# Mixer gate pieces on split weights, and the last two units' numerators ahead of the output-gate tiles

## What is computed

```python
mod = (jax.nn.silu(cond) @ ada_w + ada_b).astype(x.dtype).reshape(cond.shape[0], N_MOD, 1, D_MODEL)
sh1, sc1, gt1, sh2, sc2, gt2 = [mod[:, i] for i in range(N_MOD)]
h = rms_norm(x, norm_g[0]) * (1 + sc1) + sh1
y, st = mixer_sublayer(h, st, w_in, ...)
x = x + gt1 * rms_norm(y, norm_g[1])
h = rms_norm(x, norm_g[2]) * (1 + sc2) + sh2
a = dwconv_centred(h @ ffn_up, ffn_conv)
val, gate = jnp.split(a, 2, axis=-1)
y = (jax.nn.silu(gate) * val) @ ffn_down
x = x + gt2 * rms_norm(y, norm_g[3])
```

## Time and profile before

| what | value |
|---|---|
| device time, median of 3 runs | 873.22 us (873.04 to 874.27) |
| profiled execution: device time | 871.22 us |
| profiled execution: span | 869.5 us |
| mean granted TensorE clock | 0.976 of full speed |
| PE busy | 821.0 us, 94% of the span |
| PEld, DVE, ACT, POOL busy | 724.7, 531.2, 350.8, 86.1 us |
| line 1486 (unsplit gate pieces) in the chain that ended last | 2% of the span |

### The profile page before, as it was taken

One profiled execution on the slowest core, in us unless ns is written; L12 is line 12 of the kernel. 1 busy time (PEld: TensorE's weight loads), 2 busy tenths in 40 slices (PEclk: granted clock), 3 DMA queues, 4 the chain that ended last, 5 costly groups with the idle time before them and its releaser, 6 DMA issues.

```text
span 869.5 us, 13027 instructions
## 1 busy us (share of the span) xinstructions
PE 821.0 (94%) x4891; PEld 724.7 (83%) x4891; DVE 531.2 (61%) x763; ACT 350.8 (40%) x555; POOL 86.1 (10%) x118
## 2 busy tenths in 40 slices
PE   3679999999999979899999999999999999999996
PEld 2569999988976568659999999999999958888785
DVE  3873185797868557896555555555565564445854
ACT  3683252323111224783434343424333343335542
POOL 2630003121210026120000000000000000000000
PEclk8789999999999989999999999999999999999999
DMA  9872117578514684454222323132222063332662
GB/s 294 276 205 73 49 51 206 148 131 156 164 55 121 194 271 129 145 145 123 73 76 69 93 58 91 51 94 72 72 72 72 24 217 121 121 121 98 215 207 85
DMA packets 99951, 109.54 MB, mean 126 GB/s; under 512 B 7000, under 2 KB 79864, under 8 KB 99656
## 3 DMA queue, kind: packets, MB, share of 16 engines
q1 hardware_dynamic: 94103, 95.77, 36.7%
q0 software_dynamic: 3952, 11.53, 5.2%
q10 hardware_dynamic: 1856, 1.71, 0.6%
HBM read 106.19 MB, written 2.82 MB: 125 GB/s over the span
## 4 chain that ended last, share of the span: by engine, by line
PE 83%; DVE 7%; DMA 5%; issue 3%; ACT 3%; SPq 0%; ACTq 0%; DVEq 0%
PE PAIR L1530 47%; PE PAIR L1707 21%; PE PAIR L1540 3%; PE PAIR L1486 2%; DMA RAW<-in_ada_w_dram 2%; PE PAIR L1501 2%; DVE WLO L1030 2%; ACT WHI L790 1%; PE PAIR L1667 1%; PE PAIR L1643 1%; PE PAIR L1662 1%; DMA RAW<-in_w_out_dram 1%; PE PAIR L1678 1%; DVE T L1387 1%; DMA RAW<-in_w_in_dram 1%
## 5 line engine op out<-in xcount | busy, mean ns | idle before, releaser
L1530 PE MATMUL PAIR<-Hhi,WHI 128*128 128x320 f32 x960 | 224.7, 313 | 4.5 <-DVE Hlo L1370 3.5
L1530 PE MATMUL PAIR<-Hlo,WHI 128*128 128x320 f32 x960 | 222.5, 310 | 0.0
L1530 PE MATMUL PAIR<-Hhi,WLO 128*128 128x320 f32 x960 | 222.4, 310 | 0.0
L1030 DVE TENSOR_TENSOR WLO<-RAW,WHI 128x1024 fp32r<-128x1024 f32 (+1 forms) x115 | 146.4, 1284 | 61.9 <-ACT WHI L790 57.1
L1530 PEld LDWEIGHTS PAIR<-Hhi,WHI 128*128 128x128 f32 x960 | 161.9, 189 | 6.6 <-issue 6.3
L1530 PEld LDWEIGHTS PAIR<-Hlo,WHI 128*128 128x128 f32 x960 | 162.6, 189 | 0.0
L1530 PEld LDWEIGHTS PAIR<-Hhi,WLO 128*128 128x128 f32 x960 | 162.2, 189 | 0.0
L790 ACT ACTIVATE WHI<-RAW 128x1024 fp32r<-128x1024 f32 (+1 forms) x115 | 119.1, 1049 | 41.7 <-DMA RAW<-in_ada_w_dram 14.4
L1707 PE MATMUL PAIR<-WHI,ASHI 128*128 128x512 f32 x300 | 95.9, 401 | 9.7 <-DVE GATE L1081 5.1
L1707 PE MATMUL PAIR<-WLO,ASHI 128*128 128x512 f32 x300 | 95.3, 399 | 0.0
L1707 PE MATMUL PAIR<-WHI,ASLO 128*128 128x512 f32 x300 | 95.2, 399 | 0.0
(11 more groups left out here) (218 smaller groups left out, 835.8 us busy)
## 6 DMA issues: line engine op xcount, KB each, us to landing
RAW<-in_ada_w_dram SPq DMA_DIRECT2D x48, 512.0 KB, 4.5
RAW<-in_ffn_up_dram SPq DMA_DIRECT2D x44, 512.0 KB, 3.7
RAW<-in_ffn_down_dram SPq DMA_DIRECT2D x44, 512.0 KB, 3.3
RAW<-in_w_in_dram SPq DMA_DIRECT2D x20, 512.0 KB, 4.8
RAW<-in_w_out_dram SPq DMA_DIRECT2D x16, 512.0 KB, 5.2
WE<-weight_rows POOLq DMA_DIRECT2D x20, 128.0 KB, 4.8
out_dram<-X SPq DMA_DIRECT2D x5, 512.0 KB, 5.6
X<-in_x_sample_dram POOLq DMA_DIRECT2D x4, 512.0 KB, 6.0
```

The source lines that it names most:

```text
L1030: dve.tensor_tensor(WLO[:, u % RING, 0:w], RAW[:, u % RING, 0:w], WHI[:, u % RING, 0:w].bitcast(F32), ALU.subtract).then_inc(lo_split, 1)
L1530: last = pe.matmul(t[:, 512 * half:512 * half + HALF], w[:, n_or_slot, cols(k)], h[:, k, HALF * half:HALF * half + HALF], start=(k == 0 an ...
```

## The change

Units of pieces 4 and 5 are no longer raw: ScalarE and VectorE split all eight, and TensorE runs `split_rows` on them (16 matmuls of 512 columns for each piece, CONDHL by WHI and WLO). Pieces 10 and 11 stay as they were. In PLAN the steps behind `pl 1` are put in another order: `p2 4` and `ada 5` come first, then `C 8` and `C 9`, then both output-gate tiles. VectorE's product for `o 0`, which stood behind `C 9`, is now in step `o 0`. Step `p2 5` moves into the output projection, behind its third chunk, and uses PAIR3. By the rule of turns, `ada 4` still has PAIR0, `p2 4` now has PAIR0, `ada 5` PAIR1, `o 0` PAIR0 and `o 1` PAIR1.

What the splitting steps are given follows from `goal`: step `ad 11` now splits the first two units of piece 4 (50 and 51, in the list of all units), step `pz 1` the third (52), step `ada 4` the fourth (53) and three units of piece 5 (54 to 56), step `ada 5` the last of piece 5 (57), both output-gate tiles' (58, 59) and the first of the output projection (60). Before, `ad 11` and `pz 1` had nothing to split, `ada 4` one unit (`o 0`), and `ada 5` three.

```diff
-    ("B", 9), ("pl", 1), ("C", 8), ("o", 0), ("p2", 4), ("ada", 5), ("C", 9), ("o", 1), ("p2", 5)]
+    ("B", 9), ("pl", 1), ("p2", 4), ("ada", 5), ("C", 8), ("C", 9), ("o", 0), ("o", 1)]
...
-PLAN_OUT = (k_steps(0, KC) + [("epi", 0)] + B_OUT[0:1] + [("epi", 1), ("nrm", 0)] + B_OUT[1:2] + [("nrm", 1)]
+A_OUT = k_steps(0, KC)
+PLAN_OUT = (A_OUT[0:3] + [("p2", 5)] + A_OUT[3:] + [("epi", 0)] + B_OUT[0:1] + [("epi", 1), ("nrm", 0)] + B_OUT[1:2] + [("nrm", 1)]
...
-            ("out", "ada", 10): 2, ("out", "p2", 10): 2, ("down", "ada", 11): 0, ("down", "p2", 11): 0}
+            ("out", "p2", 5): 3, ("out", "ada", 10): 2, ("out", "p2", 10): 2, ("down", "ada", 11): 0, ("down", "p2", 11): 0}
...
         def raw_unit(n):
-            return UNITS[n][0] == "ada"
+            return UNITS[n][0] == "ada" and UNITS[n][1] > 5
...
             def ada(key, p):
-                take_rows(key, 512, key[:-2] + ("p2", p))
+                take_rows(key, 512, ("p2", 4) if p == 4 else ("out", "p2", p) if p < 11 else ("down", "p2", p))
...
                         last.then_inc(c_read, 1)
                         dve.wait_ge(c_read, UPD.index((g, d)) + 1)
-                    if n == len(MUNITS) - 1:
-                        output_gate(0)
...
-                elif kind == "o" and n:
+                elif kind == "o":
                     output_gate(n)
...
             def split_rows(s):
...
-                n = len(AD_BLOCKS[s[1]])
+                n = 4 if s[0] == "ada" else len(AD_BLOCKS[s[1]])
...
             def mix(s):
                 kind, n = s
-                if kind == "ada":
-                    ada(s, UPTO[s] - 4)
-                elif kind == "ad":
+                if kind in ("ada", "ad"):
                     split_rows(s)
...
                 elif s[0] == "p2":
-                    piece2(("out",) + s, ("out", "ada", s[1]))
+                    piece2(("out",) + s, ("ada", 5) if s[1] == 5 else ("out", "ada", s[1]))
```

## The result

The change makes the kernel slower: 876.37 us against 873.49 us, medians of 20 runs each, 2.9 us apart. The ratio is 1.0041 with a 95% interval of 1.0025 to 1.0057, some 3.6 us, and so far apart are the means too: five of the twenty runs after took 880.3 to 882.1 us, the others 874.0 to 878.1. Forecast were 873.6 us, 870.1 to 875.9, and "no change" as the likeliest case. The profiled execution after took 875.58 us (span 873.8, mean granted clock 0.975 against 0.976); it is not one of those five.

What follows compares the result with a forecast made beforehand. TensorE was taken as the bound (83% of the span), so its waits and work count. Gone 13.4 us, new waits and half clock 13.4, some 0.3 for hand-overs: net +0.3, 873.6 us, range 870.1 to 875.9.

Steps and rivals of the forecast that it cites:

- The three waits: New TensorE waits: 1.55 us before `pz 1`, about 6.8 inside piece 4, 2.2 before piece 5.
- The output gap: TensorE's 5.08 us idle before the output projection, forecast to go.
- the gap and its restart: Output projection start: 5.08 us of idle time and 1.85 lost at half clock behind it, both forecast to go.
- Step `ada 4`: Piece 4: TensorE waits about 6.8 us for unit 53's split, then restarts at half clock for 4.0 us, 1.9 lost.
- the bound of 3.0: Behind the 6.8 us wait: half clock costs between nothing and all of 3.15 + 0.93 halved, about 3.0 us.
- Step `ada 5`: Piece 5: TensorE waits 2.2 us for ScalarE's copy of PAIR1, then 0.9 for unit 57's split.
- the second one (0.9): Inside piece 5, after three quarters: TensorE waits 0.9 us for VectorE's split of unit 57.
- the second fall: Rival: clock falls at the wait before `ada 5`, piece 5 and unit 8 lose 1.5 us: 875.1; chance 0.15.
- What it removes: Pieces 4 and 5 save 6.5 us, output gap 5.08, its half clock 1.85: 13.4 gone; moving `p2 5` worth nothing.
- Clock kept: Rival: restart behind piece 4's wait gets 2.4 GHz at once, all behind it 1.9 us earlier: 871.7; chance 0.18.
- Fourth quarter in time: Rival: unit 53 split with the third, piece 4's 6.8 us wait vanishes, 3.4 us less: 870.2; chance 0.07.
- The warning that the prediction cited: Skill's "HAM oscillation", applied to `ada 4`: don't begin a matmul group before all operands are there, so the clock stays up.

Runs made afterwards that it cites:

- the fourth quarter in time: The change, with unit 53 split at `B 8` and TensorE doing unit 7's numerators ahead of piece 4: 874.02 us, ratio to before 1.0006.
- the splits alone: The kernel before with pieces 4 and 5 split but the old list of steps and `p2 5` ahead of the projection: 875.39 us, ratio 1.0033.
- the filled version: The change, fewer splits at `ad 11`, unit 53 at `B 8`, unit 7 before piece 4, `o 0` before `p2 4`, `p2` on 128 rows: 865.18 us, ratio 0.9914.

## Why the prediction was wrong

**What held.** The three waits were found in the lists by counting what stands on VectorE and ScalarE, and they came out nearly as worked out: 1.46 us ahead of `pz 1` (1.55 forecast), 6.79 in piece 4 behind line 1031 (6.8), and one behind ScalarE's copy ahead of piece 5. The output gap went, the projection started without a pause at 1.00, and GpSimd's sums delayed nothing. That the splits save 6.5 and the gap and its restart 6.9 held as well.

**Where the sum failed.** Three terms, all of the clock:

- *Step `ada 4`*: "restart at half clock for 4.0 us", taken from the restart at 309.03, where 512-column matmuls follow. Here unit 7's matmuls of 128 columns follow, and it was 8.9 us: 3.9 lost in place of 1.9, a term mis-sized by 2.0. It reaches past the bound of 3.0 that the prediction gave it. That bound does not follow from its own terms either: 3.15 + 0.93 of work at half clock loses 4.1 and not 3.0, and the state update (1.09) was left out.
- *Step `ada 5`*: because TensorE came later, its wait was 1.31 and not 2.2, and the second one (0.9) was covered by the slow matmuls: 1.8 less than forecast. But the second fall, a rival with a chance of 0.15, came and cost 1.7. Its condition was wrong too: a wait of 2.5 us or an unfinished first fall should have decided, yet the clock fell behind 1.31, and with full rows in `p2` it held behind 1.25 and 0.62. The trace before already spoke against a condition on the wait alone, with a wait of 3.27 us and a clock of 1.00 behind it:

```profile
362.57 0.70 PE L1707 MATMUL PAIR<-WHI,ASHI 128*128 128x512 f32 x2 [3.27 <-DVE ASLO L1355]
```

```profile
364.00:366.00 2.00, 2.00 (x13) 1.64 (x13) 1.97 (x4) 0.00 (x0) 0.00 (x0) 1.00 0.55 145
```

- *"What it removes"*: "`p2 5` costs 1.91 on TensorE at either place, so its move is worth nothing by itself". This is the step that failed in kind. In its old place the 5.08 us gap stood there anyway; in the new place, inside a dense projection, it is followed by 3.3 us at half clock, 1.7 lost. The trace before showed just that behind `p2 11`, inside the down projection; the prediction had costed the move by the instruction's own duration and left out what the same instruction does where it already stands among dense matmuls.

Against the forecast that is +2.0 - 1.8 + 1.7 + 1.7 = +3.6 us; the forecast net was +0.3, and 3.7 were measured in the traces. The sum of these terms and the small rest (`pz 1` itself took 7.31 in place of 7.03) reaches 4.2, half a microsecond over.

**The rivals.** "Clock kept" did not come. "Fourth quarter in time" was priced at 3.4 us under the forecast sum; the run of it lies 3.1 under the kernel after (1.0041 - 1.0006 of 873.5). That the price came out so near is partly luck, since the run also changed TensorE's order; what it showed is that VectorE's next share was already waiting behind the split. The warning that the prediction cited (the page gives it for loops that wait for DMAs) fits here: the pause inside piece 4 brought the clock down to 0.50.

The Trainium skill (TensorE: Matmul & The Clock Gate, section "Why this matters for your kernels") ties a drop of the clock in the middle of a kernel to idle gaps between bursts of matmuls. The first fall agrees with it, behind 6.79 us; the third does not, since TensorE was never idle ahead of it, and the measurement decides.

**What stays open.** When a `p2` with four rows brings a fall. Inside the projection `p2 5` was followed by one in all five traces that have it there with four rows, and in none of three with full rows. `p2 11`, among dense matmuls without a pause, was followed by one in only three of seven traces with four rows (the kernel before, the kernel after, the fourth quarter in time); in the other four the clock stayed at 1.00, and so it did in all four with full rows. Behind `p2 4` with four rows it stayed up in the kernel before and in the run with the splits alone, where no pause follows, and fell in the four traces in which a pause of 1.31 to 5.31 us follows and the first fall was over or had not come. So full rows kept the clock up in each of these places, four rows bring the fall only in some, and no run tells what decides. With one trace of most kernels chance can't be told from cause here: a wait of 3.25 to 3.58 us in the output projection stands in all eleven traces, and a fall comes with it in eight. Open are also the length of the first fall (8.9 to 21.7 us behind the same instructions) and the dip that is left in the filled version (265 to 275); its wait of 1.25 us is no longer than others that left the clock up.

## What to carry to other kernels

Cost a moved instruction by what the trace shows around the same instruction where it already stands in such company, not by its own duration alone. When a wait in a dense stretch is found, ask what TensorE does right behind it (with small matmuls there the half clock lasted 8.9 us and more, in place of 4.0 to 5.6) and what its neighbours' queues will hold next: removing one wait moved it, while filling the time with work that was ready, with full rows in `p2`, won 0.9%. Where matmuls with few rows of operands stand between dense ones, zero rows are worth a trial; here they cost nothing.

## What the runs showed of the hardware that was not expected

- Four matmuls on 4x512 operands, with no pause ahead of them or behind, can be followed by about 3.3 us at the lower clock (327.9 to 331.2 in the kernel after, and behind `p2 11` in the kernel before), though not every time. With 128 rows, zeros in the added ones, they take 1.72 us in the chain in place of 1.91 (filled version), and the clock stayed at 1.00 behind them in every such place.
- The time at the lower level behind the restart that ends a wait of 6.8 us was 5.6 us with 512-column matmuls there and 8.9 us with four of these and then matmuls of 128 columns; behind a wait of 6.94 us and the latter it was 21.7. The Trainium skill (TensorE: Matmul & The Clock Gate, Part 1) counts the warm-up in time and not in matmuls; no single time fits these restarts.
